# Hybrid decoder block with a mixture of experts: the unscaled stream is gathered, the token table is fp16, the last pair stands behind the loop, and TensorE works on constants in two waits

## The reference

```
x2 = x + mixer(rms_norm(x))                        # the "stream"
h  = rms_norm(x2)                                  # x2 * rstd[token] * norm_ffn_w[channel]
group  = top-1 of softmax(h @ w_group + b_group)   # 4 groups
expert = top-2 of the 8 experts of that group, weights = group weight * softmax of the two
for each expert e and its tokens:                  # 32 experts, 1024 (token, expert) assignments
    y = (silu(h @ w_gate[e]) * (h @ w_up[e])) @ w_down[e]     # 1024x512, 1024x512, 512x1024
x3  = x2 + sum over the two experts of weight * y
out = rms_norm(x3) * norm_final_w
```

## Time and profile before

| | us |
|---|---|
| median of 3 runs | 1114.82 (1112.35 to 1114.94) |
| profiled execution: time | 1115.29 |
| profiled execution: span | 1113.4 |
| TensorE busy | 1026.9 (92%) |
| VectorE busy | 423.7 (38%) |
| ScalarE busy | 288.1 (26%) |

### The profile page before, as it was taken

One profiled execution on the slowest core, in us unless ns is written; L12 is line 12 of the kernel. 1 busy time (PEld: TensorE's weight loads), 2 busy tenths in 40 slices (PEclk: granted clock), 3 DMA queues, 4 the chain that ended last, 5 costly groups with the idle time before them and its releaser, 6 DMA issues.

```text
span 1113.4 us, 12927 instructions
## 1 busy us (share of the span) xinstructions
PE 1026.9 (92%) x4667; PEld 657.8 (59%) x4667; DVE 423.7 (38%) x733; ACT 288.1 (26%) x484; POOL 70.8 (6%) x118
## 2 busy tenths in 40 slices
PE   4998999999999999999994799999999999898982
PEld 3887688888888888888884333333333333333331
DVE  4236146634542333554427123333333222323225
ACT  6241355444333334622212011111111011101112
POOL 0464000000000000000000000000000000000000
PEclk9998999999999999999997699999999999999995
DMA  7313122222222222216809599999999999999961
GB/s 266 114 39 108 44 76 76 76 76 76 76 76 76 95 95 90 100 53 201 351 26 376 235 421 421 420 422 421 420 421 420 421 415 422 421 420 418 420 279 77
DMA packets 59751, 263.29 MB, mean 236 GB/s; under 512 B 8948, under 2 KB 9012, under 8 KB 35128
## 3 DMA queue, kind: packets, MB, share of 16 engines
q1 hardware_dynamic: 56824, 256.36, 58.2%
q0 software_dynamic: 2304, 4.20, 1.0%
q10 hardware_dynamic: 576, 2.10, 0.5%
HBM read 262.64 MB, written 4.19 MB: 240 GB/s over the span
## 4 chain that ended last, share of the span: by engine, by line
PE 60%; DMA 32%; DVE 5%; issue 2%; ACT 1%; SPq 0%; DVEq 0%; POOL 0%; POOLq 0%; ACTq 0%
PE pj L449 43%; DMA raw_moe<-in_w_up_dram 13%; DMA raw_moe<-in_w_down_dram 9%; DMA raw_moe<-in_w_gate_dram 9%; PE pj L637 4%; PE pj L663 3%; PE cb L417 2%; PE cb L673 1%; PE cb L674 1%; DVE h L1278 1%; PE cb L495 1%; PE cb L469 1%; DMA xt<-in_x_dram 1%; PE cb L525 0%; DMA xg<-h_scratch,tok_now 0%
## 5 line engine op out<-in xcount | busy, mean ns | idle before, releaser
L637 PE MATMUL pj<-raw_moe,xT 128*64 128x512 f32 x1024 | 232.4, 602 | 18.6 <-DMA raw_moe<-in_w_up_dram 10.3
L1040 DVE TENSOR_TENSOR wl<-raw_mix,wh 128x1024 fp32r<-128x1024 f32 x88 | 108.2, 1235 | 194.8 <-ACT wh L767 194.6
L637 PEld LDWEIGHTS pj<-raw_moe,xT 128*64 128x64 f32 x1024 | 75.0, 138 | 161.1 <-issue 161.1
L1350 DVE TENSOR_TENSOR x<-x,cb 128x512 f32<-128x512 f32 x120 | 77.1, 684 | 172.8 <-PE cb L674 172.8
L449 PE MATMUL pj<-wh,hTh 128*128 128x512 f32 x320 | 132.6, 414 | 5.4 <-DVE hTl L1068 2.7
L449 PE MATMUL pj<-wl,hTh 128*128 128x512 f32 x320 | 127.3, 398 | 0.0
L449 PE MATMUL pj<-wh,hTl 128*128 128x512 f32 x320 | 127.0, 397 | 0.0
L767 ACT ACTIVATE wh<-raw_mix 128x1024 fp32r<-128x1024 f32 x88 | 92.4, 1056 | 116.3 <-PE pj L449 104.5
L663 PE MATMUL pj<-raw_moe,hf 128*64 128x512 f32 x512 | 116.9, 598 | 0.0
L449 PE MATMUL pj<-hTh,wh 128*128 128x512 f32 x192 | 81.0, 422 | 1.3 <-ACT rvo L799 1.3
L449 PE MATMUL pj<-hTh,wl 128*128 128x512 f32 x192 | 75.9, 395 | 0.0
(11 more groups left out here) (274 smaller groups left out, 1236.7 us busy)
## 6 DMA issues: line engine op xcount, KB each, us to landing
raw_moe<-in_w_gate_dram SPq DMA_DIRECT2D x64, 1024.0 KB, 9.8
raw_moe<-in_w_up_dram SPq DMA_DIRECT2D x64, 1024.0 KB, 10.2
raw_moe<-in_w_down_dram SPq DMA_DIRECT2D x64, 1024.0 KB, 9.7
raw_mix<-in_w_in_dram SPq DMA_DIRECT2D x32, 1024.0 KB, 5.0
raw_mix<-in_w_ret_branch_dram SPq DMA_DIRECT2D x4, 1024.0 KB, 4.9
raw_mix<-in_w_mlstm_branch_dram SPq DMA_DIRECT2D x4, 1024.0 KB, 5.5
raw_mix<-in_w_out_dram SPq DMA_DIRECT2D x4, 1024.0 KB, 5.4
xt<-in_x_dram SPq DMA_DIRECT2D x4, 512.0 KB, 5.2
```

Of the source, the lines that this page charges most:

```text
L637: mm = nc.tensor.matmul(pj[a * CAP:(a + 1) * CAP, up, :], xT[:, 4 * half + k, a * CAP:(a + 1) * CAP], raw_moe[(m + a) % MOE_RAW][:, k, :], ...
L1040: V.tensor_tensor(wl[:, q % RING, :, :], raw_mix[n % MIX_RAW][:, 2 * (q % 2):2 * (q % 2) + 2, :], wh[:, q % RING, :, :].bitcast(F32), ALU. ...
L1350: V.tensor_tensor(part, part, cb[:, 2 + g % 2, :], ALU.add).then_inc(c_add, 1)
```

## The change

- `h2` is no longer computed. The stream `x2` itself is stored to `x_scratch` by SP, ahead of chunk 8, and the gather reads that. The scaling by `norm_ffn_w` moves into VectorE's copy of `xT` (both halves are VectorE's now); the scaling by rstd, now the third column of `now`, moves into the sigmoid and into the two products of `silu`. Channels are split so that each half of the channels is transposed with a stride of 4, and the gate product's first half needs only the first half of `xT`.
- The comparison with the slots is made twice, with 64 columns: in fp16 for the token table, in fp32 for the weights. The token table is an fp16 product. The table of weights (and rstd) moves ahead of the first pair; its product waits for `ww_ok`.
- `keep_busy(5)` behind the logits and `keep_busy(2)` ahead of the first transposes multiply constants into a bank that nothing reads.
- For pairs 0 and 1 the gather takes its column of `tok_tab` without a copy.
- The last pair of the last round stands behind the outer loop on all engines, with an order of its own (`last_pair`): all combinations of the pair before come ahead of `down`. The last 12 chunks are issued behind SP's outer loop. The second half of `down` finishes one column half first.
- The final norm is done for two tiles at a time, behind all adds.

The diff, cut to its core:

```diff
@@ sync
-            sp.wait_ge(full[3], BLOCKS)
+            for t in range(TT):
+                sp.wait_ge(free[t], BLOCKS)
+                sp.dma_start(x_dram[t * P:(t + 1) * P, :], x2[:, t, :]).then_inc(st_in, 16)
             for m in range(8, 16):
                 moe_chunk(m, 0, 0, False)
...
             with sp.Fori(1, ROUNDS, 1) as r:
                 with sp.If(most > r * CAP):
                     round_chunks(r)
+            extra = sp.value_load(cnt[0:1, 1:2], min_val=0, max_val=ROUNDS - 1)
+            for m in range(LAST_CHUNKS, R_CHUNKS):
+                moe_chunk(m, extra, 0, True)
@@ tensor
+            def keep_busy(n):
+                for _ in range(n):
+                    nc.tensor.matmul(pj[:, 3, :], kc[:, K_IDENT:K_IDENT + P], kc[:, K_RMASK:K_RMASK + 512], start=True, stop=True)
+            keep_busy(5)
             pe.wait_ge(hot_in, 1)
...
+            def last_pair(r):
+                n = PAIRS - 1
+                N = r * PAIRS + n
+                gate_or_up(r, 0, n, 0, 0)
+                gate_or_up(r, 0, n, 0, 1)
+                gate_or_up(r, 0, n, 1, 0)
+                combine(N - 1, range(0, 2))
+                gate_or_up(r, 0, n, 1, 1)
+                combine(N - 1, range(2, 4))
+                turn_h(N)
+                combine(N - 1, range(4, 8))
+                down(r, 0, n, 0)
+                down(r, 0, n, 1)
...
                 for n in range(2 * TT):
-                    m = nc.tensor.matmul(cb[:, 2, 0:NE], at_slot[:, n // TT, n % TT, :], what[:, n // TT, n % TT, :], start=n == 0, stop=n == 2 * TT - 1)
-                m.then_inc(tab_ps, 1)
+                    for a in range(2):
+                        m = nc.tensor.matmul(cb[a * CAP:(a + 1) * CAP, 2, 0:PAIRS], at16[:, n // TT, n % TT, :], what[:, n // TT, n % TT, a:NE:2],
+                                             start=n == 0, stop=n == 2 * TT - 1)
...
+                pe.wait_ge(at_ok, r + 1)
+                pe.wait_ge(ww_ok, 1)
+                for n in range(2 * TT):
+                    k, t = divmod(n, TT)
+                    for a in range(2):
+                        m = nc.tensor.matmul(cb[a * CAP:(a + 1) * CAP, 3, 0:NE], at_slot[:, k, t, :], wrhot[:, k, :, t * NE + a:(t + 1) * NE:2],
+                                             start=n == 0, stop=n == 2 * TT - 1)
...
+                if isinstance(r, int):
+                    keep_busy(2)
                 turn_x(N0, 0)
                 turn_x(N0, 1)
@@ scalar
+            def pair(N, last=False, first=False):
+                act.wait_ge(now_ok, N + 1)
+                act.wait_ge(g_f, N * 2 + 2)
+                nc.scalar.activation(sg[:, :], pj[:, 0, :], ACT.Sigmoid, scale=now[:, 2:3]).then_inc(sg_ok, 1)
@@ vector
-            for t in range(TT):
-                for a in range(2):
-                    cols = slice(512 * a, 512 * (a + 1))
-                    m = V.scalar_tensor_tensor(h2[:, t, cols]..., x2[:, t, cols]..., stat[:, 2, t:t + 1], wrow[:, cols]..., ALU.mult, ALU.mult)
...
+            dve.wait_ge(lg_ps, 1)
+            V.tensor_copy(iot[:, :], kc[:, K_SLOT:K_SLOT + CAP]).then_inc(it_ok, 1)
...
+            def x_copy(N, part):
+                dve.wait_ge(xT_ps, N * 2 + (part + 1))
+                ks = slice(4 * part, 4 * part + 4)
+                V.tensor_tensor(xT[:, ks, :], cb[:, part, :]..., nwc[:, ks]..., ALU.mult).then_inc(xT_ok, 1)
...
-            V.memset(rden[:, 0:1], 0.0).then_inc(fin_y, 1)
+            extra = dve.value_load(cnt[0:1, 1:2], min_val=0, max_val=ROUNDS - 1)
+            pair(extra * PAIRS + (PAIRS - 1), last=True)
```

More of the change, by code:

```diff
@@ L377, in round_chunks @@
                         moe_chunk(m, r, i, True)
-                for m in range(MOE_RAW + SP_LOOPS * 2 * MOE_RAW, R_CHUNKS):
+                for m in range(MOE_RAW + SP_LOOPS * 2 * MOE_RAW, LAST_CHUNKS):
                     moe_chunk(m, r, 0, True)
@@ L703, in moe_round @@
                 turn_h(N0)
-                pe.wait_ge(ww_ok, 1)
-                for n in range(2 * TT):
-                    m = nc.tensor.matmul(cb[:, 3, 0:NE], at_slot[:, n // TT, n % TT, :], rt[:, 1 + n // TT, (n % TT) * NE:(n % TT + 1) * NE], start=n == 0, stop=n == 2 * TT - 1)
-                m.then_inc(wt_ps, 1)
                 down(r, 0, 0, 0)
@@ L711, in moe_round, with pair @@
                 down(r, 0, 0, 1)
-                def pair(i, n, last=False):
+                def pair(i, n):
                     N = N0 + i * LOOP_PAIRS + n
@@ L719, in pair @@
                     gate_or_up(r, i, n, 1, 1)
-                    if not last:
-                        turn_x(N + 1, 0)
+                    turn_x(N + 1, 0)
                     turn_h(N)
@@ L724, in pair @@
                     down(r, i, n, 0)
-                    if not last:
-                        turn_x(N + 1, 1)
+                    turn_x(N + 1, 1)
                     combine(N - 1, range(4, 6))
@@ L733, in moe_round @@
                         pair(i, n)
-                for n in range(1 + LOOP_PAIRS * PE_LOOPS, PAIRS):
-                    pair(0, n, n == PAIRS - 1)
+                for n in range(1 + LOOP_PAIRS * PE_LOOPS, PAIRS - 1):
+                    pair(0, n)
             moe_round(0)
@@ L973, in _ @@
             nc.scalar.activation(stat[:, 1, 0:TT], rt[:, 6, 0:TT], ACT.Sigmoid)
+            def pair(N, last=False, first=False):
+                act.wait_ge(now_ok, N + 1)
+                act.wait_ge(g_f, N * 2 + 2)
+                nc.scalar.activation(sg[:, :], pj[:, 0, :], ACT.Sigmoid, scale=now[:, 2:3]).then_inc(sg_ok, 1)
+                if last:
+                    nc.scalar.activation(stat[:, 1, 0:TT], stat[:, 0, 0:TT], ACT.Sqrt)
+                act.wait_ge(ht_ps, N + 1)
+                nc.scalar.activation(hf[:, :, :].rearrange("p f n -> p (f n)"), cb[:, 1, :], ACT.Copy).then_inc(hf_ok, 1)
+                if not first:
+                    act.wait_ge(c_ps, N * 8)
+                for c in range(2):
+                    act.wait_ge(y_f[c], N * 2 + 2)
+                    nc.scalar.activation(yh[:, c * 512:(c + 1) * 512], pj[:, 2 + c, :], ACT.Copy, scale=now[:, 1:2]).then_inc(yh_ok, 1)
@@ L999, in moe_round @@
-                x_copy(N0)
-                pair(N0, first=True)
+                if not isinstance(r, int):
+                    pair(N0 - 1, last=True)
+                pair(N0, first=isinstance(r, int))
                 with act.Fori(0, PAIRS - 2, 1) as i:
                     pair(N0 + i + 1)
-                pair(N0 + PAIRS - 1, last=True)
             moe_round(0)
@@ L1331, in weights @@
                 gw, ee, dd = rt[:, 7, 24:24 + TT], rt[:, 6, 0:TT], rt[:, 7, 32:32 + TT]
+                for k in range(2):
+                    V.tensor_tensor(wrhot[:, k, 1, :].rearrange("p (t n) -> p t n", n=NE), tiles(1 + k, NE),
+                                    stat[:, 2, 0:TT].unsqueeze(2).to_broadcast([P, TT, NE]), ALU.mult)
                 own(V.reduce_sum(gw, tiles(5, NG), AX.X))
@@ L1408, in moe_round @@
-                pair(N0, first=True)
+                    V.tensor_copy(cnt[:, 0:1], rt[0:1, 7, 40:41])
+                    own(V.tensor_scalar(rt[0:1, 7, 48:48 + ROUNDS - 1], kc[0:1, K_LIMIT:K_LIMIT + ROUNDS - 1], rt[0:1, 7, 40:41], None, ALU.is_lt))
+                    own(V.reduce_sum(rt[0:1, 7, 41:42], rt[0:1, 7, 48:48 + ROUNDS - 1], AX.X))
+                    V.tensor_copy(cnt[:, 1:2], rt[0:1, 7, 41:42]).then_inc(cnt_ok, 1)
+                V.tensor_scalar(slot_tab[:, :, 0], cb[:, 2, 0:PAIRS], float(NO_TOKEN), None, ALU.add)
@@ L1409, in moe_round @@
+                dve.wait_ge(wt_ps, r * 2 + 2)
+                V.tensor_copy(slot_tab[:, :, 1:3].rearrange("p n c -> p c n"), cb[:, 3, 0:NE].rearrange("p (c n) -> p c n", c=2)).then_inc(wt_ok, 1)
+                x_copy(N0, 0)
+                x_copy(N0, 1)
+                pair(N0, first=isinstance(r, int), bare=True)
                 with dve.Fori(0, PAIRS - 2, 1) as i:
                     pair(N0 + i + 1)
-                pair(N0 + PAIRS - 1, last=True)
             moe_round(0)
```

264 lines of the change are left out of this document (125 added, 139 removed).

## The result

The changed kernel takes 1115.84 us (median of 20 runs, 1114.86 to 1119.7), the kernel before took 1112.64 us beside it on the same chips (20 runs; one of them took 2672.41 us, which the median doesn't feel). The ratio is 1.0036 with a 95% interval of 1.0024 to 1.0047: slower by a third of a per cent, where 1.3% faster had been forecast. The profiled execution of the changed kernel took 1115.3 us with a span of 1113.5 us, practically that of before (1115.29 and 1113.4 us); it is one of the changed kernel's shorter executions.

The account below looks back on a forecast made before the run. The prediction took the stream of weights to bound the MoE, leaving only the two ends to gain: 1115.3 − 7.6 (front) − 7.2 (back) = 1100.5, less 0.5 for the median: 1100 us, range 1093 to 1107.

Parts of the forecast that it names:

- What bounds the loop: MoE loop: the stream of weights bounds it, about 31 us a pair at 420 GB/s; change 0.
- The front: Routing chain from the logits to the first used weight chunk: 7.6 us gained, ends 2.7 and 11.9.
- the weight table: Front, on TensorE ahead of the gather's transposes: 32 instructions on half-width tiles, bounds 1.9 and 7.3 us, 3.7 taken.
- The lower end of the front: Front with everything at half clock and upper prices: transposes at 618.9 us, first chunk used at 628.4, 2.7 us gained.
- SP's detour: SP's walk through the untaken rounds before the last 12 chunks: 5 to 6 us, costing 0, at most 1 us.
- TensorE's detour: TensorE's walk through seven untaken rounds ahead of the last pair: 5.6 us, of which 3.8 reach the end.
- a long detour: After the branch the last pair's code isn't at hand; back gives 1 to 3.5 us, about 1105 us; chance 0.09.
- the lower end of the back: Kernel's end: 3.5 us gained, with a detour twice as long or TensorE at half clock again.
- The tail: Last pair's gates to the end: final adds and norm end at 1103.1 us against 1110.35 us.

Follow-up runs that it names:

- empty rounds: Changed kernel with the seven tests of rounds 1 to 7 kept, each body only one semaphore increment: 1100.84 us, ratio 0.9883.
- the stream under the old end: Kernel before with ten more 1 MB loads, which nothing reads, behind its last chunk: 1114.07 us, ratio 0.9999.
- the changed kernel shifted by 228: Changed kernel with 228 semaphore increments that nobody waits for at the start of TensorE's program: 1130.21 us, ratio 1.0141.
- the kernel before shifted by 128: Kernel before with 128 semaphore increments that nobody waits for at the start of TensorE's program: 1126.58 us, one execution.

## Why the prediction was wrong

**What bounds the loop: right.** DMA share 1.00 and 417 GB/s late in the loop, TensorE 27.90 us busy of 31 for 27.72 before.

**The front: right.** Forecast 7.6 us, measured 8.1 in this profile and 6.2 to 6.5 in those in which chunk 18 goes out 39.2 to 39.5 us behind the last eviction. Counted from the last eviction: `lg` 4.5 us earlier (4.6 forecast), the token table done 8.2 us earlier (7.9), the copy of the column gone (1.1 us from table to issue; 1.0 taken), the gather 8.7 us under the stream (8 taken), the transposes 5.3 us earlier (5.6), from there to chunk 18 6.7 us (7.5 taken). Two terms were off without harm: the weight table took 1.92 us, not 3.7, and TensorE waited 2.6 us for the gather, where both were forecast to end together. (The lower end of the front, 2.7 us, doesn't follow from its own bounds: 608.8 + 7.3 + 4.5 gives transposes at 620.6 us, not 618.9.) The clock in detail, windows of the changed kernel:

```profile
594.00:596.00 2.00, 2.00 (x3) 0.68 (x2) 1.75 (x12) 0.21 (x1) 0.66 (x1) 0.50 1.02 426
598.00:600.00 2.00, 1.71 (x4) 0.41 (x3) 1.79 (x8) 1.08 (x2) 0.00 (x0) 1.00 1.03 434
600.00:602.00 2.00, 0.52 (x14) 0.41 (x14) 1.71 (x8) 0.61 (x2) 0.00 (x0) 1.00 1.00 422
...
604.00:606.00 2.00, 0.31 (x6) 0.34 (x8) 1.79 (x11) 0.00 (x0) 1.19 (x1) 0.50 0.96 401
...
612.00:614.00 2.00, 0.36 (x3) 0.39 (x4) 0.00 (x0) 0.00 (x0) 0.00 (x0) 1.00 0.93 389
614.00:616.00 2.00, 1.98 (x10) 1.29 (x10) 1.29 (x2) 0.00 (x0) 0.00 (x0) 0.52 0.11 45
...
618.00:620.00 2.00, 2.00 (x12) 0.75 (x10) 0.00 (x0) 0.00 (x0) 0.00 (x0) 1.00 0.26 78
```

The clock fell to 0.50 at 594 us under the fillers themselves, which filled TensorE's time (busy 2.00 of 2.00 us). It was back at full speed in 598 to 602 us, at 0.50 again in 604 to 606 us, at full speed in 612 to 614 us, when TensorE was nearly idle, and fell once more for the transposes and the first gates. Without fillers it stayed at 0.50 from 594 to 618 us, and still the token table was written only 0.4 us later (21.2 us behind the last eviction, against 20.8) and chunk 18 went out 0 to 2 us later. What each of the two groups of fillers buys wasn't measured apart. Ahead of the fall to 0.50 in 604 to 606 us TensorE had waited for most of 600 to 602 us (busy 0.52 us). Ahead of the fall at 594 us it had not: it was busy 4.00 of the 4 us from 592 to 596 us. What makes the clock fall these runs don't show.

**SP's detour: too small, without effect.** It was put at 5 to 6 us, and at 0 to 1 us of cost. SP had issued its last chunk of pair 14 by 1029.5 us and issued the next at 1041.25 us, 11.7 us later. 5.3 us of that are one stall, here in the chain of waits of the changed kernel:

```profile
1030.58 0.06 SPq L410
1030.64 5.32 issue
```

It is taken for a wait for code too: with empty rounds the same stretch is 5.6 us, and SP's seven branches take 3.0 us from first to last in place of 9.3. The four chunks in flight ran out, and the stream had its hole (64 GB/s in 1035 to 1040 us). It cost nothing only because TensorE stood longer. The trace of before had this stall; SP's branch there takes 9.1 us from first to last, and the second comes 5.6 us behind the first:

```profile
L403 SPq COMPARE_BRANCH  x7: 50/50/55, 1071.0 to 1080.1; - x7
```

**TensorE's detour, "the 5.0 us read above and one more load of a count, 5.6 us": the step that failed.** It was 21.8 us. The 5.0 us were VectorE's (its seven iterations; it releases the old combination), and TensorE's own detour was taken to be like it. This one term makes the miss: the forecast's own sum with 21.8 in place of 5.6 us gives 1116.2 us, and 1115.84 us was measured.

"Nothing in the trace prices it", the prediction said of a long detour, and that was not so. The branch's row in the trace of before has one jump of 3.4 us, and TensorE's seven tests take 8.0 us there (1082.5 to 1090.5 us). But this reading would have given 8.0 us and not the 22.8 us that they take in the changed kernel (1042.8 to 1065.6 us). The other 14.8 us are nearly all in two terms. In the middle of the stream the first jump takes 6.5 us (as with the stream under the old end: 6.0), 3.1 us more. And the second wait, 11.7 us, goes with where the code happens to lie (7.4 us with idle memory; absent in the changed kernel shifted by 228, 6.9 us in the kernel before shifted by 128), which no row of before could show. The rival "a long detour" named this term, with 0.09 and a price of a few microseconds. Its price leaned on the lower end of the back, 3.5 us for a detour twice as long; by the prediction's own sum such a detour leaves 7.2 − 5.6 = 1.6 us.

**The tail: right in kind.** From the last pair's gates to the end of the span the forecast had 44.9 us (1106.2 − 1061.3), measured 46.4. The missing 1.5 us go with the clock: after 22 us of standing the first 48 gate and `up` instructions took 12.66 us in place of three times 3.65, with the clock at 0.50 until 1071 us. From the last add to the last product it was 7.6 us, as forecast (7.7).

With all other terms as they were, a detour of 5.6 us would have given the forecast of 1100 us: no rounds at all measured 1094.23 us, the tests without code 1100.84 us. That the second is so near is partly luck: its two executions are 4.5 us apart.

**What stays open.** Which addresses make the second wait: three shifts and the run without fillers agree with the place of the code as its cause, but where the code of each program lies wasn't worked out, and the shifted programs are also late by up to 23.6 us. And why that wait is nearly twice the first; three transfers in place of one is what the queue shows. That the transfers beside a jump are the code it waits for is read from their kind and their times, and from the jumps themselves: up to 12.4 us over the rounds' code, 0.37 us at most with the bodies empty. Whether SP's stall depends on the place of its code wasn't tried.

## What to carry to other kernels

Before work is moved behind a loop that is skipped at run time, read the branch's own row on that engine's sequencer, and not the idle time of an engine that waits there for another. Here that row held a jump of 3.4 us that cost nothing: it began 2.7 us before the array was done, and VectorE's release came later still. It took 6.5 us beside the stream. Nor is that row enough, as the second wait shows: time one version with the loop left out and one with its bodies empty, before building on the new place. Skip all untaken rounds with one test, not one test a round: here that edit turned 0.4% slower into 1.3% faster, and with the last pair back in the round into 1.65%. When an edit has an effect far from where it was made, compare a run in which the code is only shifted, before any story about the work itself.

## What the runs showed of the hardware that was not expected

- The first jump over the rounds' code on TensorE: 3.4 to 4.2 us with idle memory (4 to 5 GB/s), 6.0 to 6.7 us beside the stream (392 to 426 GB/s). A second long jump, in four of the kernels and gone or there when the code was shifted: 6.9 and 7.4 us (7 GB/s), and 11.7 and 12.4 us under the stream (416 and 408 GB/s). All further jumps over the same code: 0.22 us. Each long first jump had one 16 KB transfer of the kind "instruction" beside it, each second one three.
- 128 instructions that do nothing, at the start of the program, made the end of the kernel before 4.0 us longer, while 192 changed it by 0.2 us (one execution of each).
- The seven tests with empty bodies took 0.8 us each on TensorE (1047.6 to 1052.4 us for six of them).
- A semaphore increment on TensorE, one after the other, costs 0.15 us (64 more of them, 9.8 us).
- The first gather of 128 rows of 4 KB took 8.7 us beside the full stream; that of before took 5.4 us as its stream was ending.
